# Dropping the all-zero TensorE products from the banded attention layer of a two-block transformer kernel

## What is computed

```python
def swa_mixer(h, wq, wk, wv, q_norm_w, k_norm_w, sinks, wo):
    q = rms_norm_2((h @ wq).reshape(b, l, kv, grp, d), q_norm_w) * (d ** -0.5)
    k = rms_norm_2((h @ wk).reshape(b, l, kv, d), k_norm_w)
    v = (h @ wv).reshape(b, l, kv, d)
    ...
    s_meta = jnp.einsum('bnikgd,bjkd->bnkgij', qb, km)
    s_band = jnp.einsum('bnikgd,bnjkd->bnkgij', qb, kband)
    p = sink_softmax(jnp.concatenate([s_meta, s_band], -1), sink)
    orr = (jnp.einsum('bnkgim,bmkd->bnikgd', p[..., :N_META], vm)
           + jnp.einsum('bnkgij,bnjkd->bnikgd', p[..., N_META:], vband))
    return jnp.concatenate([om, orr], 1) @ wo
```

## Time and profile before

| | |
|---|---|
| median of 3 runs | 1796.87 us (1796.28 to 1800.49) |
| the profiled execution | 1799.65 us, span of the trace 1797.8 us |
| TensorE busy | 1600.5 us (89%) |
| VectorE busy | 1212.3 us (67%) |
| ScalarE busy | 838.7 us (47%) |
| GpSimd busy | 366.8 us (20%) |
| mean granted TensorE clock | 0.973 of full |
| attention stretch of the layer | 1457 to 1593 us of the span |

### The profile page before, as it was taken

How to read it: one execution, slowest core, us unless ns; L and a number is a source line. 1 busy time by engine, 2 the same in 40 slices (tenths; PEclk the granted TensorE clock), 3 DMA queues, 4 the chain that set the end, 5 groups by cost and what they waited for, 6 DMA issues and landing times.

```text
span 1797.8 us, 24074 instructions
## 1 busy us (share of the span) xinstructions
PE 1600.5 (89%) x9314; PEld 1199.8 (67%) x9325; DVE 1212.3 (67%) x2403; ACT 838.7 (47%) x1703; POOL 366.8 (20%) x327
## 2 busy tenths in 40 slices
PE   7978998689887778878888999999999989999999
PEld 6868998554532223222342788989999866589999
DVE  6576566688888888544655689577675456567764
ACT  5545645346354444333443563345554344445542
POOL 1010011245444445433443004010001100010000
PEclk9889999899999999999999999999999998999999
DMA  6313352699999999999999222134545421035544
GB/s 261 120 71 114 141 188 94 279 386 422 427 426 427 427 427 417 428 426 428 427 427 417 73 96 95 47 118 166 181 145 175 155 94 48 3 116 188 186 155 153
DMA packets 63593, 421.15 MB, mean 234 GB/s; under 512 B 8180, under 2 KB 11512, under 8 KB 15608
## 3 DMA queue, kind: packets, MB, share of 16 engines
q0 software_dynamic: 36864, 268.45, 35.5%
q1 hardware_dynamic: 23952, 148.70, 23.1%
q10 hardware_dynamic: 2664, 2.47, 0.4%
HBM read 418.54 MB, written 1.05 MB: 233 GB/s over the span
## 4 chain that ended last, share of the span: by engine, by line
PE 65%; DMA 13%; DVE 12%; ACT 8%; issue 2%; POOL 0%; SPq 0%; ACTq 0%; DVEq 0%
PE bank L336 63%; DMA uv<-in_uv,idx 12%; DVE lows L399 3%; ACT dg L348 2%; DVE uv L1393 2%; ACT L348 1%; PE bank L2563 1%; DMA slabs<-in_w_in 1%; PE bank L341 1%; ACT acts L348 1%; ACT wp L344 1%; ACT wf L344 1%; DVE t L352 0%; ACT L349 0%; DVE cacc L352 0%
## 5 line engine op out<-in xcount | busy, mean ns | idle before, releaser
L336 PE MATMUL bank<-uv,dg 128*128 128x512 f32 x1024 | 493.5, 617 | 104.8 <-ACT dg L348 102.1
L336 PEld LDWEIGHTS bank<-uv,dg 128*128 128x128 f32 x1024 | 181.8, 192 | 405.6 <-ACT dg L348 245.0
L1393 DVE CUSTOM_DVE_ANT_0 uv<-uv,htok 128x1024 f32<-128x1024 f32 x256 | 313.1, 1223 | 169.8 <-DMA uv<-in_uv,idx 167.2
L1507 POOL DMA_INDIRECT uv<-in_uv,idx x256 | 287.7, 1124 | 374.8 <-PE bank L336 324.2
L399 DVE TENSOR_TENSOR lows<-slabs,wp 128x2048 fp32r<-128x2048 f32 (+1 forms) x78 | 167.7, 2150 | 51.5 <-ACT wp L344 51.3
L336 PE MATMUL bank<-hn,lows 128*128 128x272 f32 (+2 forms) x704 | 200.9, 285 | 0.0
L514 POOL TENSOR_TENSOR sqT<-sqT 128x256 f32<-128x256 f32 (+1 forms) x42 | 46.7, 1111 | 679.8 <-ACT sqT L348 677.5
L348 ACT ACTIVATE acts<-acts 128x1 f32<-128x1 f32 x256 | 51.3, 200 | 282.4 <-DVE acts L1393 282.1
L344 ACT ACTIVATE wp<-slabs 128x2048 fp32r<-128x2048 f32 (+1 forms) x78 | 140.6, 1803 | 82.3 <-DMA slabs<-in_dn 27.4
L336 PEld LDWEIGHTS bank<-hn,lows 128*128 128x128 f32 x704 | 132.7, 188 | 0.0
L336 PE MATMUL bank<-hh,lows 128*128 128x272 f32 x448 | 132.3, 295 | 0.0
(11 more groups left out here) (383 smaller groups left out, 3021.9 us busy)
## 6 DMA issues: line engine op xcount, KB each, us to landing
slabs<-in_up SPq DMA_DIRECT2D x44, 1024.0 KB, 4.8
slabs<-in_w_in SPq DMA_DIRECT2D x28, 1024.0 KB, 4.9
slabs<-in_dn SPq DMA_DIRECT2D x32, 704.0 KB, 4.1
slabs<-in_wkv SPq DMA_DIRECT2D x8, 1024.0 KB, 4.9
slabs<-in_w_out SPq DMA_DIRECT2D x8, 1024.0 KB, 4.8
slabs<-in_pq SPq DMA_DIRECT2D x8, 1024.0 KB, 4.8
slabs<-in_wq SPq DMA_DIRECT2D x4, 1024.0 KB, 4.8
slabs<-in_wo SPq DMA_DIRECT2D x4, 1024.0 KB, 4.8
```

What stands on the lines that cost most here:

```text
L336: ins = T.e.matmul(pr[2] if len(pr) > 2 else out, pr[0], pr[1], start=(start and k == 0), stop=(stop and k == len(pairs) - 1), skip_group_ ...
L1393: V.e.tensor_tensor_reduce(u_, u_, htok[:, n, :], 1.0, 0.0, ALU.mult, ALU.add, acts[:, n, e_:e_ + 1]).then_inc(*V.up("dot", q))
L1507: G.e.indirect_dma_start(uv[q % NU][:, :], None, d["uv"][:, :], bass.IndirectOffsetOnAxis(ap=idx[:, n, e_:e_ + 1], axis=0)).then_inc(s_uv[ ...
```

## The change

The zero products are taken out, and with them the tile, the memset and the helper that chose their banks. The list of steps is otherwise the same in content and order. Nothing is put in their place.

```diff
-                    idle = sbuf(ph, "idle", [P, 640], BF16)
...
                 out += [("att", it, s) for it, s in r] + extra
-                if not [x for x in extra if x[0] == "sq"]:
-                    out.append(("warm", 0, 0))
             return out
...
-        SWA = with_next_piece([y for x in FIRST for y in ([x, ("warm", 0, 0)] if x[0] == "qn" else [x])] + attention_plan())
+        SWA = FIRST + attention_plan()
...
-                elif x[0] == "warm":
-                    idle_tensor(*x[1:])
...
-        def idle_tensor(name, i, j):
-            was = PBANK[name, i, j][1]
-            T.wait_ge(*evac_lane(*was).at("ev", *was))
-            T.wait_ge(*G.at("idle"))
-            for _ in range(3):
-                T.e.matmul(pbank(name, i, j)[:, :], idle[:, 0:P], idle[:, P:640], start=True, stop=True, skip_group_check=True)
...
             G.stage("swa")
-            G.wait_ge(*T.at("pj", "dn0", 15))
-            G.e.memset(idle[:, :], 0.0).then_inc(*G.up("idle"))
             squares_gpsimd("fn1", T2)
```

More of the change, by code:

```diff
@@ L10 @@
 U32 = mybir.dt.uint32
-BF16 = mybir.dt.bfloat16
 ALU = mybir.AluOpType
@@ L2460, in attention_plan @@
                 out += [("att", it, s) for it, s in r] + extra
-                if not [x for x in extra if x[0] == "sq"]:
-                    out.append(("warm", 0, 0))
-            return out
[L2465 to L2474, removed]
-        SWA = with_next_piece([y for x in FIRST for y in ([x, ("warm", 0, 0)] if x[0] == "qn" else [x])] + attention_plan())
+            return out
+        SWA = FIRST + attention_plan()
         KEYS = {1: (144, [1], "mb0"), 2: (272, [1, 2], "mb1")}
```

## The result

The changed kernel takes 1807.18 us (median of 20 runs, 1799.61 to 1815.67) against 1796.82 us before (20 runs, 1789.18 to 1807.73). The ratio is 1.0056, 95% interval 1.0040 to 1.0072: slower by about 10 us, and clear of no change. Forecast was a time within 0.3% of the one before, at 1794.5 us. The measured time lies inside the range of 1784 to 1808, near its upper end, but on the other side of no change than the forecast. It is what the slower rival had said.

What follows compares the result with a forecast made beforehand. Tensor work was taken to bound the 136 us stretch. Terms -0.3 - 1.3 - 2.0 + 0 - 0.3 + 1.5 summed to -2.4 us, from 1796.87 to 1794.5 us, range 1784 to 1808.

Steps and rivals of the forecast that it cites:

- the slower rival: 1551 to 1593: clock falls and stays down; 1804.5 us at three quarters, 1809 at all; chance 0.32 with half the third rival.
- time on the chain: 1457 to 1593: zero products hold 17.7 us of the chain; 13.4 us come back with the clock as it was.
- the clock's term: 1457 to 1593 and after: each us at the lower level costs half a us, less what it hides of waits.
- four spells of 3.4 us in place of one: 1551 to 1593: 10.2 us more at the lower level, +5.1 us, of which 1 hides waits.
- from the last slab's `tw` to the transpose of `m0`: 1517 to 1533: 4.2 us gained, 2.2 lost as real work moves into the fall at 1524; sum -2.0.
- The first slab: 1457 to 1466: 1.5 us of zero products go, one new lower-clock spell costs 1.2; sum -0.3.
- From the second slab's `nq`: 1490 to 1517: -1.3 us; query thirds keep the engine in dense work, so no new fall.
- Part 4: 1533 to 1551: all 8.9 us of real work at the lower level, 2.1 of waits left, 18 us; sum 0.
- Parts 5 and 6: 1551 to 1593: 4.4 us gained, longer work at the lower level, sum -0.3; after 1593 one more spell, +1.5.
- The further spell that I put behind 1593: After 1593, a dense stage: one more lower-clock spell on full work, up to +1.7, taken as +1.5 us.
- third rival: Zero products never on the path, only the clock counts: about 1805 us; half of it shares the slower rival's 0.32.
- The signs named: 1457 to 1593: 133 to 135 us long; clock well below 0.9 from 1533 to 1551, 0.8 to 0.9 afterwards.

Runs made afterwards that it cites:

- the middle fillers: Against the kernel before, zero products kept only in the 16 warm steps between the last slab's `tw` and the first output piece: 1.0019.
- the burst: The changed kernel with 15 zero products in one block ahead of the first output piece: 1.0101 of the time before.
- the merging: Eight 16-column products of each learned-token item became two of 64: with the zero products 0.9971 of the time before, without them 1.0037.

## Why the prediction was wrong

The argument had the right two sides, time on the chain against the clock, and the right mechanism for each. The step that failed is the size of the clock's term. For 1551 to 1593 it took "four spells of 3.4 us in place of one", +5.1 us of longer real work; the real work there grew by 11.9 us. With too small a term in most of the parts ahead as well, -2.4 us became +9.1.

- **Time on the chain.** The 17.7 us of zero products did come off, by the account above 17.0. Where the time at the lower level did not grow, from the last slab's `tw` to the transpose of `m0`, I had -2.0 and it was -2.8.
- **The first slab, forecast -0.3, measured +1.8.** I allowed one spell of 3.4 us at the lower level with 2.4 us of real work in it. It was 6.8 us long (1466 to 1473), and 2.8 us of the query thirds that follow the waits ran in it.
- **From the second slab's `nq`, forecast -1.3, measured +0.2.** "No new fall" was wrong. TensorE was busy for 0.70 of the 2 us from 1504, waiting for the reciprocal, and the clock was down from 1507 to 1514. Two `warm` steps had stood at 1499 and 1500, just ahead of that wait.
- **Part 4, forecast 0, measured +3.9.** The clock was 0.50 as forecast. Two terms were too small. I took the tiny products of `m0` as bound by their number and not by the clock: they took 3.59 us there against 1.95, +1.6. And the waits were 20.00 - 16.13 = 3.9 us instead of 2.1, +1.8. Together 3.4 of the 3.9.
- **Parts 5 and 6, forecast -0.3 and +1.5, measured +7.2 and -1.3.** This is the largest miss. The zero products from 1551 to 1593 are those of part 5 and the last two steps, which stand in part 6. The sum had -12.0 us for them, +5.1 of longer real work and +6.6 of waits (12.0 less the 4.4 of gain and the 1 that was hidden). Measured over both parts are -12.0, +11.9 (in part 5, 24.8 to 36.7 us) and +6.1: the waits were right, and the clock's term was less than half of what it should have been. I counted four spells, 13.6 us, by the third of the time that the first block's mixer spends at the lower level. It was 25 of 44 us, more than half. The row from 1480 to 1490, busy for ten of ten us at 0.50, spoke for it, and I used it for the rival only. Two falls are new, at 1575 and 1589, each at or just behind a wait on VectorE where zero products had stood: 10 us together, not more than I had counted. The other 14 us are the spell that began in part 3 and went on into part 5, which the sum did not have at all. (Where the clock was full at the start of part 5, with the middle fillers and with the burst, later falls made up for most of it: 17 us at the lower level in part 5 and 6 in part 6.) The further spell that I put behind 1593 (+1.5) did not come; part 6 stands at full clock. The slower rival named this place and this mechanism, and had +7.8 us at three quarters of the work and +12.5 at all of it, against +9.1 in the trace and about +10 in the medians.
- **Slips in the working.** The third rival's sum adds 11 where its own gain of 13.4 us belongs: -2.4 + 13.4 = +11.0, 1808 us and not 1805. That would have fitted the time, but its cause is not the one: the 17.0 us that came off show that the zero products were on the path. And the rows are of two output pieces: VectorE's at 1586.31 and 1587.30 belong to the piece at 1584.76 and not to that at 1580.08, behind which the 1.24 us stand.
- **TensorE's waits on VectorE.** They did show up, as said. In part 5, behind output pieces, they are longer than before, 5.9 us in five waits, against 0.9 in two:

```profile
PE bank L334 <- DVE pt L2663: 5.9, 5, 1.9
```

- **The signs named.** The stretch 1 to 3 us shorter: it is 9.1 us longer. Part 4 well below 0.9: 0.50, right. Part 5 at 0.8 to 0.9: 0.72, outside, toward the slow side, though 25 of 44 us is not yet the two thirds that I had named there. Tensor busy time little below that of before: 131.5 against 136.9 us, right. All times ahead of the layer unchanged: 3.8 us later, within the scatter of the 14 traces. The end unchanged: right.

The rule of the Trainium skill ("TensorE: Matmul & The Clock Gate", "HAM oscillation — how this bites in real kernels") that pauses put the clock back agrees with the falls of the changed kernel: at 1466 and 1483 during waits of 2.4 and 4.5 us, at 1507 about 1 us behind a wait of 1.3 us, and at 1530.9 somewhat over 1 us behind waits of 1.5 and 0.6 us. The kernel with zero products 4 rows deep adds what the rule does not say: without any pause to speak of (0.2 of 88.5 us) the clock stays at its lower level as well. The section "Part 4: PE-mode transpose" says that transposes do not bring the clock up. That would fit part 4 after the merging, where transposes took 4.5 us and the narrow group 1.1, but no run here took the transposes away.

## What to carry to other kernels

Price a filler on TensorE by both sides: its time on the chain, and the time at the lower clock that it keeps away, at half a microsecond each, carried on into the dense work that follows. Its depth counts: 128 rows held the clock here, 4 rows did not, and nothing between was tried. A stretch of narrow products, transposes and short waits doesn't bring the clock back by itself, however busy the engine looks, so make the narrow products fewer and wider first (0.9971 here), and put fillers where the engine waits (seen in the traces, hardly in the medians). Judge such an edit by many runs: the pattern of the clock differs from one execution to the next by more than the gain (8.8 us ahead of this layer, over the same work).

## What the runs showed of the hardware

- The same product, 128 by 512 columns in bfloat16 and zero in every element, holds the clock when it is 128 rows deep (1.00 and 0.95 in parts 4 and 5 before) and does not when it is 4 rows deep (0.50 and 0.54 in the same parts, with TensorE busy for 88.3 of 88.5 us).
- The lower level lasted for 41 of 42 us with TensorE busy for 38.1 of them, two output pieces of full depth among them; with the zero products 4 rows deep it lasted for 83 of 88.5 us. A burst of 15 full-depth zero products brought it to an end within its 5.1 us.
- Very small products follow the clock too: 16 of them in the records, 16 rows deep and 16 columns wide, each with a weight load of its own, took 1.95 us at the upper level and 3.59 us at the lower.
